# One query projection for tiles 1 to 4 per head, 76 rows of the second table ahead, and the output projections in one row

## What is computed

```
x = x + concat(a_out, b_out) @ w_out                       # output projection
q = (rmsnorm(x) @ w_q).reshape(T, 8 heads, 2, 128)
s = einsum('thcd,hcnd->thcn', q, sub_keys)                 # 128 key scores, twice per head
s1, i1 = top_k(s[:, :, 0], 16);  s2, i2 = top_k(s[:, :, 1], 16)
cand = s1[..., :, None] + s2[..., None, :]                 # 256 pairs
top_s, pos = top_k(cand, 16);    eid = i1 * 128 + i2 at pos
g   = softmax(top_s)
hid = gelu(einsum('thkd,td->thk', u_tab[eid], x))          # 16384 x 1024 table
y   = einsum('thk,thkd->td', g * hid, v_tab[eid])          # 16384 x 1024 table
```

## Time and profile before

| | |
|---|---|
| median of three timed runs | 1910.77 us (1908.88 to 1916.44) |
| the profiled execution | 1924.79 us, of which 1923.0 us from its first to its last instruction |
| PE, DVE, ACT, POOL busy in it | 1465.4, 1055.3, 216.1, 1055.5 us |
| moved by DMA in it | 670.00 MB, mean 348 GB/s |

### The profile page before, as it was taken

One profiled execution on the slowest core, in us unless ns is written; L12 is line 12 of the kernel. 1 busy time (PEld: TensorE's weight loads), 2 busy tenths in 40 slices (PEclk: granted clock), 3 DMA queues, 4 the chain that ended last, 5 costly groups with the idle time before them and its releaser, 6 DMA issues.

```text
span 1923.0 us, 16500 instructions
## 1 busy us (share of the span) xinstructions
PE 1465.4 (76%) x5398; PEld 545.3 (28%) x5398; DVE 1055.3 (55%) x2879; ACT 216.1 (11%) x610; POOL 1055.5 (55%) x1119
## 2 busy tenths in 40 slices
PE   6979996678888888766767667656676667777997
PEld 3575663344443334431111111111111111111221
DVE  2256997774166645545766555667677766422000
ACT  2321214444101100011000000010000000100000
POOL 3023443332366655566676666666676666666664
PEclk9889997887999898889999999999999999999999
DMA  9587889999699889999999999999999999999997
GB/s 306 185 301 286 293 290 393 383 403 371 247 391 389 318 337 363 351 356 339 364 373 385 358 363 385 349 364 375 376 360 372 363 364 367 366 366 364 379 352 286
DMA packets 213254, 670.00 MB, mean 348 GB/s; under 512 B 19600, under 2 KB 54656, under 8 KB 213040
## 3 DMA queue, kind: packets, MB, share of 16 engines
q0 software_dynamic: 157728, 571.78, 78.9%
q1 hardware_dynamic: 55440, 97.16, 14.2%
HBM read 663.26 MB, written 5.60 MB: 348 GB/s over the span
## 4 chain that ended last, share of the span: by engine, by line
PE 32%; issue 17%; DMA 16%; POOL 14%; DVE 11%; another core or an unknown queue 8%; ACT 2%; DVEq 0%; SPq 0%; ACTq 0%; POOLq 0%
POOL area_r L1626 14%; PE bank L774 11%; DMA area_r<-in_v_tab,eidT 9%; PE bank L549 8%; PE bank L719 4%; DMA area_w<-in_v_cache 3%; DVE area_r L1469 3%; DMA area_r<-in_u_tab,eid 2%; PE bank L672 2%; PE bank L633 2%; PE bank L492 1%; PE bank L737 1%; DMA area_w<-in_w_in 1%; PE bank L546 1%
## 5 line engine op out<-in xcount | busy, mean ns | idle before, releaser
L1469 DVE CUSTOM_DVE_ANT_0 area_r<-area_r,bank 128x1024 f32<-128x1024 f32 x544 | 655.8, 1214 | 335.4 <-DMA area_r<-in_u_tab,eid 287.3
L774 PE MATMUL bank<-area_r,area_c 128*32 128x512 f32 (+1 forms) x1632 | 664.7, 614 | 224.0 <-DMA area_r<-in_v_tab,eidT 179.3
L1626 POOL DMA_INDIRECT area_r<-in_u_tab,eid x544 | 522.5, 961 | 485.4 <-DVE hid L1469 235.1
L1626 POOL DMA_INDIRECT area_r<-in_v_tab,eidT x544 | 517.4, 951 | 366.7 <-PE bank L774 151.9
L774 PEld LDWEIGHTS bank<-area_r,area_c 128*32 128x32 f32 (+1 forms) x1632 | 132.1, 109 | 730.7 <-DMA area_r<-in_v_tab,eidT 391.3
L774 PE MATMUL bank<-area_r,area_v 128*32 128x512 f32 (+1 forms) x544 | 269.9, 619 | 85.5 <-DMA area_r<-in_v_tab,eidT 64.9
L719 PE MATMUL bank<-area_t,area_w 128*128 128x128 f32 (+2 forms) x672 | 144.0, 377 | 32.5 <-ACT area_x L878 18.8
L549 PE MATMUL bank<-area_w,area_t 128*128 128x384 f32 (+1 forms) x448 | 158.0, 510 | 7.8 <-DMA area_w<-in_w_in 7.3
L719 PEld LDWEIGHTS bank<-area_t,area_w 128*128 128x128 f32 x672 | 108.2, 215 | 69.8 <-issue 53.9
L774 PEld LDWEIGHTS bank<-area_r,area_v 128*32 128x32 f32 (+1 forms) x544 | 48.9, 110 | 261.1 <-DMA area_r<-in_v_tab,eidT 136.4
L549 PEld LDWEIGHTS bank<-area_w,area_t 128*128 128x128 f32 x448 | 84.5, 192 | 71.8 <-issue 17.7
(11 more groups left out here) (168 smaller groups left out, 992.0 us busy)
## 6 DMA issues: line engine op xcount, KB each, us to landing
area_w<-in_w_q SPq DMA_DIRECT2D x21, 1024.0 KB, 7.9
area_w<-in_w_in SPq DMA_DIRECT2D x12, 1536.0 KB, 10.2
area_w<-in_k_cache SPq DMA_DIRECT2D x8, 1920.0 KB
area_w<-in_v_cache SPq DMA_DIRECT2D x8, 1920.0 KB
area_r<-in_u_tab,eid POOLq DMA_INDIRECT x544
area_r<-in_v_tab,eidT POOLq DMA_INDIRECT x544
area_w<-in_w_out SPq DMA_DIRECT2D x4, 2048.0 KB, 8.6
area_w<-in_w_in SPq DMA_DIRECT2D x2, 2048.0 KB, 17.2
```

Of the source, the lines that this page charges most:

```text
L774: mm = pe.matmul(acc[CG * g:CG * g + m, e, :], wd[g][:, c * CG:c * CG + m], v_ring[s][:, e * 512:(e + 1) * 512], start=False, stop=False, ...
L1469: vec.tensor_tensor_reduce(out=u_ring[s], in0=u_ring[s], in1=x_cur, scale=1.0, scalar=0.0, op0=ALU.mult, op1=ALU.add, accum_out=hid[t % 2] ...
L1626: nc.gpsimd.indirect_dma_start(out=ring[s], out_offset=None, in_=table, in_offset=bass.IndirectOffsetOnAxis(ap=where, axis=0)).then_inc(la ...
```

## The change

The five jobs for tile 1 alone are gone: all eight heads make their queries once, for the 416 tokens of tiles 1 to 4, and only after all output projections. The second table's lead is 76 in place of 30. PE projects tiles 1 to 4 out in a row, with eight calls of `weigh` behind each half, and the norms of tiles 1 to 4 stand on DVE ahead of the routing and not among the dots. ACT follows PE's order. `s_early`, the place for the scores of the short jobs, falls away.

```diff
-NORM_AT = {SLOTS + 24: 2, SLOTS + 30: 3, SLOTS + 37: 4}
-V_LEAD = 30
-EARLY = 5
+V_LEAD = 76
...
-        JOBS = ([(h, [0]) for h in range(HEADS)] + [(h, [1]) for h in range(EARLY)]
-                + [(h, list(range(1, NT))) for h in range(EARLY, HEADS)] + [(h, list(range(2, NT))) for h in range(EARLY)])
+        JOBS = [(h, [0]) for h in range(HEADS)] + [(h, list(range(1, NT))) for h in range(HEADS)]
...
             project_out(1, 1, 8)
-            weigh_first(8)
-            turn_xn(1)
-            pe.wait_ge(xnT_ready, 4)
-            pe.wait_ge(x2_ready, 4)
-            for i in range(HEADS, EARLY_END):
-                queries(i)
-                weigh_first(4)
-                key_scores(i)
-            for c in range(2):
-                pe.wait_ge(q_copied[c], EARLY_END)
-            pe.wait_ge(s_ready, scores_through(EARLY_END - 1))
             for t in range(2, NT + 1):
                 if t < NT:
-                    project_out(t, 0, 4)
-                    project_out(t, 1, 4)
-                if t >= 3:
-                    turn_xn(t - 1)
+                    project_out(t, 0, 8)
+                    project_out(t, 1, 8)
+                turn_xn(t - 1)
             pe.wait_ge(xnT_ready, 2 * NT)
             pe.wait_ge(x2_ready, 2 * NT)
-            queries(EARLY_END, (4, 4))
-            for i in range(EARLY_END, len(JOBS)):
+            queries(HEADS, (4, 4))
+            for i in range(HEADS, len(JOBS)):
                 if i + 1 < len(JOBS):
-                    queries(i + 1, (4, 4) if (i - EARLY_END) % 2 else (4, 0))
+                    queries(i + 1, (4, 4 * ((i + 1) % HEADS in (5, 7))))
                 key_scores(i)
             weigh_first(EID_FIRST - made[0])
...
                     i = made_dots[0]
-                    if i in NORM_AT:
-                        norm_x2(NORM_AT[i])
...
             weights(0)
-            norm_x2(1)
+            for t in range(1, NT):
+                norm_x2(t)
             dve.wait_ge(xn_ready, 2)
             set_x(1)
             go_on(routings([HEADS, HEADS + 1]))
```

More of the change, by code:

```diff
@@ L114, in build @@
         s_first = cut(area_w, RING * PIECE + D, HEADS, 2 * NKEYS)
-        s_early = cut(area_v, NT * D, EARLY, 2 * NKEYS)
         cand = cut(area_w, RING * PIECE + 3 * D, TOPK * TOPK)
@@ L335, in dots_in_group @@
             return 3 if before else 0
-        JOBS = ([(h, [0]) for h in range(HEADS)] + [(h, [1]) for h in range(EARLY)]
-                + [(h, list(range(1, NT))) for h in range(EARLY, HEADS)] + [(h, list(range(2, NT))) for h in range(EARLY)])
+        JOBS = [(h, [0]) for h in range(HEADS)] + [(h, list(range(1, NT))) for h in range(HEADS)]
         SCORED = [(t, h) for h, ts in JOBS for t in ts]
         score_at = {th: i for i, th in enumerate(SCORED)}
-        EARLY_END = HEADS + EARLY
         def job_tokens(i):
@@ L354, in s_of @@
                 return s_first[0:n, h, :]
-            return s_early[0:n, h, :] if t == 1 and h < EARLY else s_rest[0:n, t - 1, h, :]
+            return s_rest[0:n, t - 1, h, :]
         def wait_apart(engine, what, value):
@@ L1160, in _ @@
             copy_weights(0)
-            read_out(1)
-            square_x2(1)
-            copy_xnT(1)
-            for i in range(HEADS, EARLY_END):
-                copy_q(i)
-                copy_s(i)
-            for t in range(2, NT + 1):
+            for t in range(1, NT + 1):
                 if t < NT:
@@ L1170, in _ @@
                     square_x2(t)
-                if t >= 3:
+                if t >= 2:
                     copy_xnT(t - 1)
-            copy_q(EARLY_END)
-            for i in range(EARLY_END, len(JOBS)):
+            copy_q(HEADS)
+            for i in range(HEADS, len(JOBS)):
                 copy_s(i)
```

## The result

| | before | changed |
|---|---|---|
| median | 1913.61 us (1908.88 to 1920.55) | 1984.24 us (1972.82 to 1986.50) |
| profiled execution | 1924.79 us (span 1923.0) | 1982.83 us (span 1980.8) |
| moved by DMA | 670.00 MB, 348 GB/s | 664.72 MB, 336 GB/s |

The ratio is 1.0343, 95% interval [1.0304, 1.0381]: slower by 71 us between the medians, by 58 us between the profiled executions. The forecast was +48 us, 1959 us, with a range of 1930 to 1990. The changed kernel lies 6 us inside the upper end of the range.

A forecast was written before the change was run, and what follows sets the result against it. DMA engines, mostly gathers at 1.43 us, bound the kernel where full; elsewhere engine order does. First U gather 663 + gathers 257.4 + loads 8.6 + gaps 5.2 + wait 6 = 940 against 892: +48, so 1959 us; range 1930 to 1990.

The forecast's parts named there:

- idle part ahead of the first U gather: Tile 1's first U gather at 663 us, before 535; 76 V gathers, worth 109 us, in 191 us; +62 us.
- w_q loads in the stretch behind: Behind tile 1's first U gather three loads of w_q in place of ten, 2.86 us each; -20 us.
- time lost behind the first U gather, beyond gathers and loads: Small gaps of 5.2 us as before, plus a new 6 us wait of POOL; +6 us.
- The walk: PE's work from first weighing at 490.4 us through output halves, transposes and query halves; first U gather at 663 us.
- The 6 us wait for DVE: POOL waits from 673 us until DVE, routing heads 0 and 1 first, frees a buffer near 679.5; 6 us.
- I take them over: Behind tile 1's first U gather: the 5.2 us lost to small gaps before are carried unchanged into the changed kernel.
- PE holds the V gathers later too: Rival: after tile 1's first U gather, V gathers waiting for PE stop U gathers; up to +77 us, 1988; chance 0.15.
- Rows don't wait: Rival: with only V gathers queued, rows land sooner for PE's weighings; +4 to +35 us, around 1930; chance 0.18.
- The bytes decide: Rival: V lead keeps DMA full until U gathers start; 14.3 us gained, 1896; first U gather before 615; chance 0.04.
- No net effect: Rival: the late start is made up by idle time of the DMA engines later; chance 0.03.

The follow-up runs named there:

- A: Chip kind, not an edit: steady stretch at 365 to 368 GB/s, 1.43 us a gather; the kernel before at 1911 to 1929 us.
- B: Chip kind, not an edit: 397 to 404 GB/s over all runs, 1.33 us a gather; the kernel before at 1805 us.
- e14: The changed kernel with no edit, on a chip of kind B, against the kernel before: ratio 1.0302, 1858.9 against 1804.7 us.
- e10: Kernel before, tile 4's norm five dot products later, routing of tile 1's sixth head eight later, on B: ratio 0.9990, 1802.1 against 1805.1 us.

## Why the prediction was right, and where it was off

**The sign and the cause held.** Tile 1's first U gather waits for PE's whole walk, the V gathers that POOL may issue in that time don't fill it, and nothing gives the idle time back later. In the terms of the forecast, over the stretch from the first V gather to tile 2's first U gather, on A:

| term | forecast | measured (profiled executions) |
|---|---|---|
| idle part ahead of the first U gather: its delay less the V gathers at 1.43 us | 191 - 108.7 = 82.3; before 20.4: +62 | 183.3 - 108.7 = 74.6; before 63.3 - 42.9 = 20.4: +54 |
| w_q loads in the stretch behind, 2.86 us each | 3 for 10: -20 | 3 for 8: -14; on B five are worth 11.5 of 13.3 us |
| time lost behind the first U gather, beyond gathers and loads | 11 for 5: +6 | 306 - 266 = 40, before 363 - 346 = 17: +23 |
| sum | +48 | +63 |

(180 x 1.43 + 3 x 2.86 = 266, and 226 x 1.43 + 8 x 2.86 = 346. Both stretches include a wait at tile 2's first U gather, which is 5.5 us before and 7.4 after, and which the forecast left out on both sides.)

The forecast put all ten later loads of before behind its first U gather. Two of them went out ahead of it (the row at 521.55 above), so with eight the time that before loses to gaps by the forecast's own working is 357 - 346 = 11 us and not 5.2.

On B the same sum, of e14 against e10 (which is level with before, and has before's loads), is 62 for the idle part (81.2 against 18.7), -13 for the loads, +8 for the time lost behind (15.0 against 7.5): +57 us. The forecast's first two terms came on both kinds of chip. It is the last that differs, +8 on B and +23 on A.

**How near it was, and by what.** Over this stretch the sum is 15 us above the forecast: the idle part is 8 us smaller, the loads save 6 us less (the miscount), and the time lost behind is 17 us greater. The profiled executions differ by 58 us and not by 63, as the V gathers start 4.2 us sooner in the changed kernel, which the forecast did not have, and the rest is 1 us shorter. That the forecast was only 10 us off there is thus in part luck. Its largest term, the idle part, was within 8 of 62 us.

**The walk** (663 forecast, 191 us after the first V gather; 183 measured). The sets of eight weighings took 10.4 to 11.5 us, not 10.1, but for some 9 in the one behind tile 4's first half. Tile 4's second output half took 5.6 us where I had 9.8, the four transposes 4.9 us in sum where I had 9.6, and the first query half 5.85 us where I had 8.1. In these three I took a row of before whose stretch had U gathers in the queue. The twelve weighings between the query halves took 9.6 us, as forecast (7.3 and 2 for late rows).

**The 6 us wait for DVE** near 675 came as 6.60 us at 667.22.

**The step that was mis-sized** is "I take them over": the 5.2 us of small gaps behind the first U gather, carried from a stretch of 226 gathers of which 98 were V, to one with fewer V gathers. Two things stand in its place. First the turn of tile 1's row numbers. It is in PE's order behind weighing 108 in both kernels. With a lead of 30 POOL is at U gather 102 of tile 1 when it comes to V gather 108, with 76 it is at U gather 79, and the head whose row numbers are turned last is routed later than that. A change of the lead moves every point that is counted in weighings against every point that is counted in U gathers, and I had moved only the first U gather. On B moving the turn gives back 9 to 11 us, all of the +8 there. Second, on A, the late hand-overs, which hold PE and with it POOL's V gathers: POOL's waits, all causes, add up to 86 us over 226 gathers before and to 90 us over 180 gathers after. That they make the 15 us by which A's last term exceeds B's is argued from the waits in the traces; no run on A takes them away. They are in the kernel before too, only shorter: PE waits 16.6 us in five waits for ACT's copies of queries between its two first U gathers, the longest 5.6 us, against 23.9 us and 16.9 after, and 4.6 us for copies of scores, against 16.6.

**The rival "PE holds the V gathers later too"** thus came in part. I had argued against it with the number of V gathers, 52 for 98. The waits come fewer (6 for 12) and longer (42.3 us in sum for 38.6), which fits that they hang on PE's stops and not on the number of gathers. **"Rows don't wait"** fell: there is one wait in each set, and 4.6 us from issue (486.88) to weighing (491.46). By the fit in the Trainium skill, "DMA: Bandwidth & Descriptors", section "Anatomy of one DMA", 2.0 us and the bytes over 436 GB/s, an estimate for this is 3.2 us; the row of after is longer, as that of before was. **"The bytes decide"** fell by its own test, a first U gather before 615. **"No net effect"** fell by the equal times of the rest.

**Still open** is what makes a hand-over late on A. The trace shows that ACT waits for something that it puts down to no engine, that it happens while the DMA engines are full, and that on B nothing of the kind occurs at a higher DMA rate. A full queue alone is thus not enough. The records of matmuls have modelled ends, so it can't be said whether PE ends late or its signal comes late. The Trainium skill, "Perfetto Trace Analysis", section "Tensor Engine Instruction (MATMUL, LD_WEIGHTS)", says that PE's recorded end is estimated and that the semaphore is updated only when the result is acknowledged as written. The trace has the recorded end at 694.5 and ACT's start at 710.50, and no run here separates the two steps. The run meant for it fell twice on a chip that doesn't have the effect.

## What to carry to other kernels

A lead in one queue that another queue's order is built on shifts all points that are counted in the one against those counted in the other; list them all (here the first U gather, the turn behind weighing 108, the routings) and price each. Ask of work moved ahead of a start not how long it takes but how much of that time the transfers allowed meanwhile can fill: here 76 gathers filled 109 of 183 us on A, and on B four weighings per half in place of eight gave back 18 us of idle time and, as the turn came right with it, more than half of the loss. Where one issuing engine serves two rings in one order, a wait that is removed at one ring may only move to the other, as in the run with two waits later; see what holds the other ring before it is counted as a gain.

## What was not expected of the hardware

Chips of one type differ: 365 and 368 against 398 GB/s in the same 442 us of the changed kernel, 6 to 7% in the time of the kernel before. The steady stretch on A is not an even slower pace. Cut into slices of 11 us it reaches 413 GB/s in several of them and falls to 175 and 281 in others. One of these holes, in the changed kernel, holds a late hand-over: ACT's copy at 1335.66 stood 11.84 us with a wait put down to no engine, PE waited 11.03 us for it, and the DMA share fell.

```profile
1332.00:1342.00 10.00, 5.26 (x16) 1.71 (x20) 7.70 (x29) 5.27 (x10) 3.65 (x4) 0.52 0.78 279
1342.00:1344.00 2.00, 2.00 (x18) 0.57 (x12) 1.30 (x3) 0.00 (x0) 0.80 (x1) 1.00 0.04 12
```

So the 1.43 us a gather, which the prediction took for the price of the bytes, holds as a mean on A but is in part such holes; on B it is 1.33. The Trainium skill, "DMA: Bandwidth & Descriptors", section "Specifications", gives some 358 GB/s as the limit of HBM for one core, half of a stack's 716. It was no bound here, with one core at work: the traces show 368 GB/s on A and 398 on B over 442 us.
